# Expert blocks of a MoE decoder layer: four small experts in one block, fewer pairs, and a new order of the blocks

## The reference

```
lg = xt @ rg_w + rg_b;  p_top, g = top-1 of softmax(lg)          # 4 groups
v2, e = top-2 of (xt @ re_w + re_b) in group g                   # 8 experts a group
w2 = softmax(v2) * p_top
out = sum over the two experts e of (silu(x @ Wg[e]) * (x @ Wu[e]) * w2) @ Wd[e]
```

```
0 to 7:   76  38  59  38  63  79  60  13
8 to 31:  34  74  42  11  14  23  37  13 134  90  97 119  88 127  52 111 110  69  36  44  81 135 135  74
```

## Time and profile of the kernel before

| | |
|---|---|
| times, three runs | 608.02, 608.03, 610.11 us; median 608.03 us |
| the profiled execution's own time | 608.55 us |
| its span, first to last instruction | 606.5 us |
| its mean granted TensorE clock | 0.981 of full speed |
| mixers and router | 0 to about 387 us |
| blocks of the experts | about 387 to 561.8 us |
| sums, final norm, stores | 561.8 to 606.5 us |

### The profile page before, as it was taken

One profiled execution on the slowest core, in us unless ns is written; L12 is line 12 of the kernel. 1 busy time (PEld: TensorE's weight loads), 2 busy tenths in 40 slices (PEclk: granted clock), 3 DMA queues, 4 the chain that ended last, 5 costly groups with the idle time before them and its releaser, 6 DMA issues.

```text
span 606.5 us, 9765 instructions
## 1 busy us (share of the span) xinstructions
PE 571.4 (94%) x3401; PEld 473.4 (78%) x3401; DVE 439.9 (73%) x749; ACT 242.2 (40%) x389; POOL 88.5 (15%) x136
## 2 busy tenths in 40 slices
PE   8899999999999999899999995899997999999775
PEld 6799999997899889688888874777654768887222
DVE  4937997999999696746666658899731667786285
ACT  6642112222212427322222116576322567775443
POOL 4300000200000000100000000433331334431000
PEclk9999999999999999999999997899998999999889
DMA  8761210131112202455422107699989999962697
GB/s 317 150 123 38 69 36 1 36 93 35 36 36 79 105 36 69 114 203 198 157 80 93 54 36 247 215 332 404 392 329 412 407 352 395 394 241 97 209 421 299
DMA packets 52598, 111.27 MB, mean 183 GB/s; under 512 B 10867, under 2 KB 29176, under 8 KB 51449
## 3 DMA queue, kind: packets, MB, share of 16 engines
q1 hardware_dynamic: 44773, 92.18, 43.2%
q0 software_dynamic: 7168, 17.84, 8.2%
q10 hardware_dynamic: 596, 0.50, 0.3%
HBM read 96.36 MB, written 21.86 MB: 195 GB/s over the span
## 4 chain that ended last, share of the span: by engine, by line
PE 51%; DVE 17%; DMA 7%; issue 3%; ACT 2%; SPq 1%; POOL 0%; POOLq 0%; DVEq 0%; ACTq 0%
PE ps L2259 14%; PE ps L2081 9%; PE ps L2425 6%; PE ps L2364 3%; PE ps L2386 3%; PE ps L2400 3%; PE ps L2401 3%; PE ps L2402 3%; DMA at_opair_p<-scratch_out 3%; DMA at_wlater<-in_expert_w_down 3%; DVE at_mixP L1360 3%; PE ps L2496 2%; PE ps L2323 2%; DVE at_hT L1319 1%; DVE at_lnsq L1546 1%
## 5 line engine op out<-in xcount | busy, mean ns | idle before, releaser
L2081 PE MATMUL ps<-at_hT,at_ring 128*128 128x384 f32 x936 | 165.5, 333 | 0.0
L2081 PEld LDWEIGHTS ps<-at_hT,at_ring 128*128 128x128 f32 x936 | 155.9, 188 | 5.1 <-issue 5.0
L2259 PE MATMUL ps<-at_hT,at_mring 128*128 128x512 f32 (+1 forms) x432 | 102.7, 393 | 2.0 <-DVE at_mring L1514 1.3
L2259 PEld LDWEIGHTS ps<-at_hT,at_mring 128*128 128x128 f32 (+1 forms) x432 | 77.3, 182 | 21.3 <-DVE at_mring L1514 1.7
L1360 DVE SCALAR_TENSOR_TENSOR at_mixP<-at_uc,at_par,at_mixP 128x1024 f32<-128x1024 f32 x60 | 77.1, 1285 | 2.1
L2400 PE MATMUL ps<-at_whi,at_hTm 128*128 128x256 f32 x176 | 51.0, 290 | 0.0
L2402 PE MATMUL ps<-at_whi,at_hTm_lo 128*128 128x256 f32 x176 | 49.1, 279 | 0.0
L2364 PEld LDWEIGHTS ps<-sb_ident,at_xg 128*128 128x128 f32 x232 | 29.3, 192 | 18.2 <-issue 15.2
L1795 DVE TENSOR_TENSOR at_wlater_lo<-at_wlater,at_whi 128x1024 fp32r<-128x1024 f32 x30 | 36.7, 1225 | 6.0 <-ACT at_whi L988 5.1
L2425 PE MATMUL ps<-at_wlater,at_actT 128*128 128x512 f32 (+1 forms) x92 | 38.0, 597 | 0.7 <-ACT at_actT L1003 0.7
L988 ACT ACTIVATE at_whi<-at_wlater 128x1024 fp32r<-128x1024 f32 x30 | 31.6, 1055 | 7.3 <-PE ps L2402 6.5
(11 more groups left out here) (324 smaller groups left out, 919.2 us busy)
## 6 DMA issues: line engine op xcount, KB each, us to landing
at_wlater<-in_expert_w_gate SPq DMA_DIRECT2D x20, 512.0 KB, 11.1
at_wlater<-in_expert_w_up SPq DMA_DIRECT2D x20, 512.0 KB, 12.8
at_wlater<-in_expert_w_down SPq DMA_DIRECT2D x20, 512.0 KB, 15.4
at_raw<-in_w_in SPq DMA_DIRECT2D x16, 512.0 KB, 4.0
at_opair_p<-scratch_out SPq DMA_DIRECT2D x8, 1024.0 KB, 14.7
at_wfirst<-in_expert_w_gate SPq DMA_DIRECT2D x12, 512.0 KB, 9.0
at_wfirst<-in_expert_w_up SPq DMA_DIRECT2D x12, 512.0 KB, 10.0
at_wfirst<-in_expert_w_down SPq DMA_DIRECT2D x12, 512.0 KB, 12.5
```

Source lines behind the costliest of these rows:

```text
L2081: mm = pe.matmul(ps[:, bank + r, 0:t1 - t0], w[:, wpart, k * P:(k + 1) * P], hT[:, hpart, k, t0:t1], start=(m, wpart, hpart) == (0, 0, 0), ...
L2259: mm = pe.matmul(ps[0:n, b + r, :], mring[:, 1 - i % 2, mpart, k * P:k * P + n], wo[:, wpart, k, r * 512:(r + 1) * 512], start=(c, mpart, ...
```

## The change

Constants: PAIRS goes from 5 to 3, a new QUADS = 1 is a block with **four** experts of at most 32 rows, each on a quarter of the array's columns and of the block's rows; EXTRA goes from 2 to 1, one block for the rows past 128 of all four large experts, 32 rows each. NB becomes 27. The order of the blocks behind the fixed ones is no longer by class but by a string, `ORDER = "XLMLLQLMMPMPMMMMMPM"` (X extra block, L large, M mid, Q four small experts, P pair). SyncE loads the experts in the order in which the blocks first use them (`LOADS`), and a place w is now a number in that order, while VectorE's placing counts by class. VectorE has a class more to sort out, and four groups of lanes to copy for a block of four.

```diff
-FIX, PAIRS, LARGE = 8, 5, 4
+FIX, PAIRS, QUADS, LARGE, EXTRA = 8, 3, 1, 4, 1
 REST = NE - FIX
-LIGHT = 2 * PAIRS
-EXTRA = LARGE // 2
-NB = NE - PAIRS + EXTRA
+TINY = 4 * QUADS
+LIGHT = TINY + 2 * PAIRS
+LANES = LARGE // EXTRA
+NB = FIX + PAIRS + QUADS + EXTRA + LARGE + MID
+ORDER = "XLMLLQLMMPMPMMMMMPM"
+def table():
+    first = {"Q": 0, "P": TINY, "X": LIGHT, "L": LIGHT, "M": LIGHT + LARGE}
+    count = {"Q": 4, "P": 2, "X": LANES, "L": 1, "M": 1}
+    out = []
+    for k in ORDER:
+        out.append((k, list(range(first[k], first[k] + count[k]))))
+        first[k] += count[k]
+    return out
+TABLE = table()
+LOADS = list(dict.fromkeys(c for _, cs in TABLE for c in cs))
...
+def experts(r):
+    if r < FIX:
+        return [r]
+    if r >= NB:
+        return [r + NE - NB]
+    return [FIX + LOADS.index(c) for c in TABLE[r - FIX][1]]
...
             for w in range(FIX, NE):
-                e = sp.value_load(eid[0:1, w - FIX:w - FIX + 1], min_val=0, max_val=NE - 1)
+                c = LOADS[w - FIX]
+                e = sp.value_load(eid[0:1, c:c + 1], min_val=0, max_val=NE - 1)
                 sp.wait_ge(s["d_done"], done_in(w - LAP) + 1)
...
             for h in range(2):
-                do(g.iota(iox[h * 64:h * 64 + 64, :], [[2, PAIRS + EXTRA]], base=h, channel_multiplier=0, **flt))
+                do(g.iota(iox[h * 64:h * 64 + 64, 0:PAIRS], [[2, PAIRS]], base=TINY + h, channel_multiplier=0, **flt))
+            for n0, n, first, lanes in ((PAIRS, QUADS, 0, 4), (PAIRS + QUADS, EXTRA, LIGHT, LANES)):
+                for t in range(lanes if n else 0):
+                    q = slice(t * P // lanes, (t + 1) * P // lanes)
+                    do(g.iota(iox[q, n0:n0 + n], [[lanes, n]], base=first + t, channel_multiplier=0, **flt))
...
             def class_experts():
+                if QUADS:
+                    do(ts(few, rest, 32.0, None, ALU.is_le))
+                    running()
+                    do(stt(tiny, run, TINY + 0.5, few, ALU.is_le, ALU.mult))
+                    do(ts(quads, run, float(TINY), None, ALU.min))
                 do(ts(few, rest, 64.0, None, ALU.is_le))
+                if QUADS:
+                    do(tt(few, few, tiny, ALU.subtract))
...
             def place_experts():
                 do(tt(mid, mid, held, ALU.subtract))
+                if QUADS:
+                    do(tt(p_from, l_from, taken[:, REST - 1:REST], ALU.subtract))
+                    do(ts(p_from, p_from, 2.0 * PAIRS, None, ALU.add))
+                    do(ts(q_left, quads[:, REST - 1:REST], -1.0, float(LIGHT), ALU.mult, ALU.add))
+                    do(tt(mid, mid, quads, ALU.subtract))
+                    do(ts(late, mid, p_from, q_left, ALU.is_ge, ALU.mult))
+                    do(ts(pos, mid, l_from, s_left, ALU.is_ge, ALU.mult))
+                    do(tt(pos, pos, late, ALU.add))
...
+                if QUADS:
+                    do(stt(quads, quads, -1.0, mid, ALU.add, ALU.subtract))
+                    do(tt(quads, quads, tiny, ALU.mult))
+                    do(tt(held, held, quads, ALU.add))
...
-            def pair_columns(c, at_, count):
-                do(v.tensor_copy(late[0:64, :], columns(c)[0:64]))
-                do(v.tensor_copy(late[64:P, :], columns(c)[0:64]))
+            def lane_columns(c, at_, count, lanes):
+                n = P // lanes
+                for t in range(lanes):
+                    do(v.tensor_copy(late[t * n:t * n + n, :], columns(c)[0:n]))
                 pick(iox, at_, at_, count, late)
...
+            def quad_columns():
+                if QUADS:
+                    lane_columns(0, PAIRS, QUADS, 4)
             def extra_columns():
-                pair_columns(1, PAIRS, EXTRA)
+                quad_columns()
+                lane_columns(1, PAIRS + QUADS, EXTRA, LANES)
...
                     for k in range(KC):
-                        for t in range(2):
-                            n = slice(64 * t, 64 * t + 64)
+                        for t, w in enumerate(experts(j)):
+                            n = lane(j, t)
                             mm = pe.matmul(out[n], hTp[:, j % 2, k, n],
-                                           half(wexp(place(j, t)), k // 4)[:, :, k % 4, :],
+                                           half(wexp(w), k // 4)[:, :, k % 4, :],
                                            start=k == 0, stop=k == KC - 1)
```

## The result

| | before | after |
|---|---|---|
| median | 609.07 us (4 runs, 608.02 to 610.69) | 615.83 us (4 runs, 614.69 to 616.74) |
| ratio to before | | 1.0114, 95% interval 1.0092 to 1.0135 |
| profiled execution | 608.55 us, span 606.5 | 616.74 us, span 615.0 |
| last down products end | 561.8 | 572.3 |
| last weight matrix landed | 544.3 | 561.75 |

The change makes the kernel 1.1% slower, 6.8 us by the medians. I had predicted 609.1 us and a range up to 615.0. All times and ratios are of fast executions; one execution of experiment 7, of 614.81 us at a lower granted clock, was a slow one and is left out.

What follows compares the result with a forecast made beforehand. TensorE was taken to set the stage's end, with the weights only 7.0 us ahead; the gated weight stream then moved that end from 561.8 to 562.9, +1.1 us on the 608.03 median, giving 609.1 us, range 601.0 to 615.0.

Steps and rivals of the forecast that it cites:

- TensorE's saving and the tiles: Expert blocks on TensorE: two grouped steps go, -13.0 us, plus 4.8 us of waiting; a four-tile step takes 6.5.
- the two-by-two rival: Four-tile blocks: tiles served two at a time, 5.4 us more a block, up to 619.9 us; chance 0.08 including cases between.
- VectorE's additions: Added VectorE operations ahead of block 8: +4.8 us in sum, 0.5 of it absorbed by waits; bounds 3.0 and 4.8.
- The first two items: VectorE ahead of block 0's weight split: five more operations before the first gather, +1.1 us, nine more in placing, +2.0.
- Step 3: VectorE's column picking in this step of the stage: five operations become 14, +1.9 us.
- block 7's down products end 4.3 us later: TensorE at block 7: VectorE's added work delays the end of its down products by 4.3 us, to 442.0.
- The gate: SyncE's load 19, with 20 to 31 queued behind, can't be issued before block 14 ends, at 482.5 us.
- The stream behind the gate: Loads 19 to 31 plus gathered and scattered rows: 27.2 MB at 392 GB/s, 69.4 us, last landing at 552.9.
- From the last landing to the end: Splitting the last expert's weights, its products and the last two blocks' down products: 10.0 us, stage end at 562.9.
- the gates count double: Loads 17 and 18 land late, so block 14 waits 1 to 2 us; with 374 GB/s, 613 to 614 us; chance 0.25.
- The weights catch up: DMA engines use the time from 450 to 482 better, last landing 544.3 to 549.5, 600.5 to 605.7 us; chance 0.22.

Runs made afterwards that it cites:

- experiment 7: The kernel before, with its same blocks in the mixed order PMXLLXLLPMMPMMPMMPMMM and no added VectorE operations: 609.77 us, ratio 0.9991 to before.
- Experiment 8: The changed kernel with the overflow counts moved from step 6 to step 7 and the rest of them to steps 12 to 16: 614.58 us, ratio 1.0083 to before.
- experiment 9: The changed kernel with five pairs for the block of four, order PMXLLLLMMPPMMMPMMMMP, less VectorE work, overflow counts moved: 601.89 us, ratio 0.9868 to before.
- experiment 10: The changed kernel with the block of four undone and two pairs in its place, 28 blocks: 616.31 us, ratio 1.0107 to before.
- experiment 1: The kernel before with 26 small VectorE operations added on scratch columns, as many as the change adds at each place: 616.77 us, ratio 1.0099 to before.
- experiment 3: The changed kernel with ORDER XLLLLQPPPMMMMMMMMMM, the four large blocks directly behind the extra block: 611.45 us, ratio 1.0008 to before.
- experiment 4: The changed kernel with ORDER PMXLLLLMMMMQMMPMMMP, a pair and a single block ahead of the extra block: 607.80 us, ratio 0.9950 to before.
- experiment 6: The changed kernel with ORDER PMXLLLLMMMMQMMPMMMP, lane columns picked in 7 operations instead of 14, overflow counts moved to other steps: 604.49 us, ratio 0.9912 to before.

## Why the prediction was wrong

**TensorE's saving and the tiles: right.** Two grouped steps are gone, and the four tiles run at once. A four-tile block's 64 matmuls take 3.7 us (439.51 to the start of the last at 442.79, and its 0.38), as much as a pair's 32, and the step that holds those of block 13 takes 6.4 us (465.65 to 472.05), as a pair's does. So the two-by-two rival falls.

The Trainium skill, "TensorE: Matmul & The Clock Gate", section "Measured speedup vs the span model", has a speedup of 2.38 for three column tiles. The 1.4 us more a block that I had estimated from it isn't there: 3.7 us against the pair's 3.67. The measurement decides.

**VectorE's additions: right in kind, short by 3.05 us.** The first two items were right: at block 0's last weight split VectorE is at 389.32 where it was at 385.67, 3.65 us later, 3.2 by the added operations (3.1 foreseen) and 0.5 that was there before them. The timeline rows of VectorE, before and after:

```profile
385.67 1.23 DVE L1795 TENSOR_TENSOR at_wfirst_lo<-at_wfirst,at_whi 128x1024 fp32r<-128x1024 f32 x1
```

```profile
389.32 1.22 DVE L1850 TENSOR_TENSOR at_wfirst_lo<-at_wfirst,at_whi 128x1024 fp32r<-128x1024 f32 x1
```

Step 3 gave 1.6 (1.9 foreseen). I had taken 0.5 off the sum for waits that would absorb part of it, but block 6's down products are 5.4 us late (434.79 against 429.35): the 0.5 from the start, and 4.9 us of additions that nothing absorbed. And I overlooked **step 6**, whose operations are the counts of the overflow. Three more stand there, and the copy ahead of them waits 1.29 us for a scatter to land, against 0.18 before. So block 8's rows come 1.64 us late to TensorE, and block 7's down products are 1.9 us later still. The prediction's step "block 7's down products end 4.3 us later" is the first that failed: it was 7.35, by about 1.9 for step 6, 0.6 for what wasn't absorbed and 0.5 from ahead of the additions. Experiment 8 takes just the part of step 6 out.

**The gate: right.** From block 7 to the end of block 14 I counted 482.5 - 442.0 = 40.5 us. It took 443.10 + 1.98 to 486.3, 41.2 us. Block 17 waited 7.6 us, with 5 to 8 foreseen. The DMA share from 450 to 482 was 0.79, though, not the 0.5 to 0.7 that I had expected.

**The stream behind the gate: the second term that failed.** I had 27.2 MB at 392 GB/s and 1.0 for the first issue, 70.4 us. It was 27.7 MB by the three windows, in 75.5 us, 367 GB/s. While the engines were full, the rate was 399, better than I took. What I missed are the two ends: 290 GB/s in the first 8.7 us and 311 in the last 16.8, at a share of 0.83. Against 399 throughout they cost 2.4 and 3.7 us. Why the rate is so low at the start, where the share is 0.92, is open. The tail could be read from the kernel before, in the last 22 us of its own stream (windows, columns as above):

```profile
500.00:522.00 22.00, 22.00 (x149) 18.17 (x148) 17.49 (x20) 15.98 (x25) 9.89 (x8) 1.00 1.02 392
522.00:544.30 22.30, 22.30 (x152) 18.46 (x151) 17.98 (x21) 16.38 (x26) 8.45 (x7) 1.00 0.83 319
```

The 363 GB/s that I started from the earlier trace rows had this tail in it. I divided by the share of 0.97 to get "374 when full" and so took the tail out again, and then went up halfway to 412, which I had left undivided. 27.7 MB at 363 are 76.3 us, near the 75.5 measured. An average rate of a full stretch was used for a stretch with a start and an end.

**From the last landing to the end:** 10.6 us, 10.0 foreseen.

The sum of the stage: 562.9 + 3.8 (the gate, of which 3.05 come from VectorE) + 5.1 (the stream) + 0.6 = 572.4, and the profile has 572.3. Behind the stage the profile after is 2.0 us shorter (42.7 against 44.7), which no term explains; the other profiles lie between 41.5 and 44.2, so it is taken as scatter between executions.

The rival that came nearest is "the gates count double", 613 to 614 at a chance of 0.25. It was to be decided by a landing time of 9 us for loads 17 and 18. Their last matrices, issued at 468.61 and 475.11, took 10.2 and 10.4 us, and ScalarE waited for the first of them (timeline rows of ScalarE and TensorE):

```profile
478.82 1.06 ACT L1014 ACTIVATE at_whi<-at_wfirst 128x1024 fp32r<-128x1024 f32 x1 [2.68 <-DMA at_wfirst<-in_expert_w_down]
...
481.48 0.30 PE L2476 MATMUL ps<-sb_ident,at_actv 128*128 128x128 f32 x1 [0.68 <-DVE at_actv L1812]
```

The step that ends with block 14's down products takes 6.65 us (477.78 to 484.43) in place of 5.6. So its mechanism was there, with 1 us at the low end of the 1 to 2 that it gave; the steps before it were 0.3 us shorter than I had counted, and 0.75 us is left in the sum. It also had the lower mean rate, 374 in its sum against 367 measured. What it lacked is VectorE's 3.05 us, and the rest of the rate.

"The weights catch up" is wrong in its premise too: the engines did use much of the time ahead of the gate (a share of 0.81 from 440 to 490), but the 4.2 MB less that they had moved by its end, against before, had to come later, and the stream had been nearly full in the kernel before (0.97 from 473 to 544).

The bounds of the range were too narrow in two terms that lie on one chain and add. VectorE's was 4.8 us and the front was 7.35 late; the lowest rate was 374 GB/s and it was 367. With both at their far ends the prediction would have been 609.1 + 0.5 + 3.3 = 612.9 us, still short of 615.83.

The front delays here are differences of single profiles, and these scatter. The profile of before has block 0's down products earliest of all, at 394.82; experiments 7, 9 and 10, without VectorE's additions at that point, have them at 395.5 to 396.4, and the five profiles with the changed kernel's additions there at 398.2 to 400.2. So some 1 to 2 us of any such difference can be chance.

## What to carry to other kernels

When two resources are both nearly full over a stage (here TensorE and the weights, 7 us apart), count a change on the chain of gates that the slower one depends on. A microsecond added ahead of the gate cost about all of itself (experiments 1 and 10). Behind the gate TensorE was idle for 13.4 of 75.5 us, so one saved there should be worth nothing; no run tested that alone. An order that uses many buffers early and frees them late starves the queue: here it paid to let the blocks that free the four experts follow at once (experiment 3), though not every mixed order gained (experiment 7). Take a rate from a stretch that begins and ends as the one to be predicted does, or add its ends. And a planner that computes on the chip is part of the bill: look at each step that it grows in, not at those alone that the feature is named after.

## What the runs showed of the hardware

Two things I had not expected. First, four fp32 matmuls on four column tiles of 32 start within 20 ns, and it is 0.21 to 0.24 us from one group of four to the next, as it is with two tiles.

Second, TensorE's granted clock at the start of the stage differs from profile to profile, and the front moves with it. In the window from 386 to 396 us the granted clock was 1.00 (2.4 GHz throughout) in the kernel before, and a mean between the two levels, 2.4 and 1.2 GHz, of 0.83 in the changed kernel, 0.55 in experiment 1, 0.66 in experiment 4 and 0.83 in experiment 7. The rows, in this order:

```profile
386.00:396.00 10.00, 9.41 (x68) 8.32 (x69) 8.29 (x10) 7.00 (x11) 2.61 (x2) 1.00 0.97 297
```

```profile
386.00:396.00 10.00, 8.07 (x52) 7.31 (x53) 8.18 (x22) 4.93 (x7) 2.87 (x3) 0.83 0.92 285
```

```profile
386.00:396.00 10.00, 8.36 (x39) 7.59 (x40) 7.07 (x19) 3.28 (x4) 2.86 (x3) 0.55 0.89 280
```

```profile
386.00:396.00 10.00, 7.61 (x42) 7.05 (x43) 7.02 (x20) 3.17 (x4) 3.17 (x5) 0.66 0.92 278
```

```profile
386.00:396.00 10.00, 8.85 (x62) 8.67 (x63) 7.30 (x8) 5.76 (x9) 2.71 (x2) 0.83 0.99 308
```

VectorE's later tables are not the reason by themselves: in experiment 7 its last split of block 0 starts at 385.87, as before, and the clock fell all the same. Nor do TensorE's waits for its first two blocks of gathered rows explain it. They were 1.64 and 0.68 us before, at 1.00; 1.12 and 0.90 in experiment 7, at 0.83; 1.34 and 1.27 in experiment 10, at 1.00; 2.55 and 0.32 in the changed kernel, at 0.83; and 2.39 and 0.65 in experiment 1, at 0.55.

What the fall goes with can be seen in a comparison. The changed kernel and experiments 3, 4, 6 and 8 have the same operations up to this point. From VectorE's last split of block 0 to block 0's down products it is 9.1 to 9.3 us in the changed kernel and in experiments 3 and 6 (clock 0.83 in all three), and 10.5 us in experiments 4 and 8 (0.66 in both): 1.2 us. In the kernel before it was 9.15 us (1.00), and in experiment 1 it was 11.5 us (0.55), 2.3 us more. These are single profiles, and why the clock differs between kernels that are the same up to there is open.
